# Attention output products of a two-layer encoder trunk: three rounded passes in place of fp32, with the probabilities and values split into high and low parts

## The chip, the cores and the metric

The kernel runs on one core of a Trainium2 chip. The metric is the device time in microseconds (us) of one execution. PE is TensorE, ACT is ScalarE, DVE is VectorE, POOL is GpSimd and SP is SyncE; PEld is TensorE's loading of weights.

## The reference

Two request groups of 256 and 512 tokens go through the same two layers of width 1024. Each layer has a mixer (a Hyena part and a Mamba-2 part), a cross-attention into 256 memory tokens of each group, and a squared-ReLU MLP. The change is in the cross-attention alone:

```
def memory_cross_attention(u, mem_n, w_q, w_kv, w_o):
    q = (u @ w_q).reshape(b, L, XA_HEADS, XA_HEAD_DIM)           # 4 heads of 256
    kv = (mem_n @ w_kv).reshape(b, m, 2, XA_HEADS, XA_HEAD_DIM)  # m = 256
    k, v = kv[:, :, 0], kv[:, :, 1]
    s = jnp.einsum("bqhd,bkhd->bhqk", q.astype(f32), k.astype(f32)) * (XA_HEAD_DIM ** -0.5)
    a = jax.nn.softmax(s, axis=-1)
    o = jnp.einsum("bhqk,bkhd->bqhd", a, v.astype(f32)).reshape(b, L, D_MODEL).astype(u.dtype)
    return o @ w_o
```

The outputs are fp32.

## The kernel before

Both groups are laid side by side as one axis of T = 768 tokens (6 tiles of 128; SEGS are the columns 0 to 256 and 256 to 768). Activations lie with the features on the partitions. Every engine has its own program, written out by hand in the order in which it is to run; engines wait for one another by semaphores alone. An engine that waits holds up all that stands behind in its list.

Most products of the kernel take operands that are split in two rounded parts (F32R, "hi" and "lo", lo = value - hi). The helper `three` issues three matmuls, hi x hi, hi x lo and lo x hi, into one PSUM bank. Other products, among them the scores and the output products of the attention, take fp32 operands with one call, which the chip's program holds as two instructions.

The attention of a layer runs over four heads. TensorE's list for head h is:

- T(h), line 1527: 12 transposes of the normalised probabilities `prob` into `tr_bank(0)`, `tr_bank(1)` (the two banks of PSUM tensor G[0]) and `tr_bank(2)` (a bank of M[1]). It waits for `p_nrm` (normalised) and for `o_lo` of the first output of head h-1, since that output lies in G[0].
- S(h+1), line 1060: 12 products for the scores of the next head, into M, for heads 0 to 2.
- O(h), line 1538: 8 products of `vt` (values, stationary) and `probT` (moving) into G[0] and G[1], 4 of 256 and 4 of 512 columns. They wait for `p_tc`. In the last head the two 256-column halves come first.

ScalarE's list for head h is: three copies of the transposed probabilities into `probT` (line 888, `p_tc`), the six exponentials of head h+1 (line 857, each followed by the reading of its sum), then B_hi of both outputs (line 894, waits for `o_mm`). Ahead of head 0 stand eight halves of weight chunks (lines 881 and 882) that the products behind the attention use.

VectorE's list is: the softmax of head h+1 (line 2150 maximum, 2151 scaling, 2156 reciprocal, 2157 normalisation, in the order maximum 0, maximum 1, normalise 0, maximum 2, normalise 1, normalise 2), then B_lo of both outputs (line 2196, waits for `o_hi`, raises `o_lo`). Behind the last head TensorE waits for `o_lo` and goes on with weight tiles (line 1108).

Of the kernel before, what the change touches and what calls it, by code (L numbers as in the profile page):

```python
# [21 lines left out]
F32R = mybir.dt.float32r  # L22
ALU = mybir.AluOpType
# [4 lines left out]
P = 128  # L28
# [83 lines left out]
def build_trunk(nc, xT, memT, wstream, dft, fw3, params, consts, yT):  # L112
    ctx = ExitStack()
    with ctx:
# [90 lines left out]
        qfa = place("qfa", [P, 6, T], oE + 12288)  # L205
        qfb = place("qfb", [P, T], oA + 45056)
        prob = [place(f"prob{i}", [P, TT, NMEM], oA + 32768 + 6144 * i) for i in range(2)]
        probT = [place(f"probT{i}", [P, 2, T], oE + 32768 + 6144 * i) for i in range(2)]

        relu = [place(f"relu{i}", [P, T], oE + 3072 * i) for i in range(2)]  # L210
        hidf = [place(f"hidf{i}", [P, T], oE + 6144 + 3072 * i) for i in range(2)]
# [89 lines left out]
        def par_(name, i=0, n=1, rows=P):  # L301
# [21 lines left out]
        xg_mix, xg_mlp = sem("xg_mix"), sem("xg_mlp")  # L323
        st_sum, st_var, st_std, st_rc, st_bc, st_rbc = (sem(n) for n in (
            "stat_sum", "stat_var", "stat_std", "stat_rcol", "stat_bc", "stat_rbc"))
        pre_sq = sem("pre_square")
        wdt_h, wdt_l, dt_mm = sem("wdt_hi_done"), sem("wdt_lo_done"), sem("dt_taken")
        dt_p, dt_f, dt_t = sem("dt_product"), sem("dt_scaled"), sem("dt_turned")
        conv_x, silu_d = sem("conv_for_silu"), sem("silu_done")
# [231 lines left out]
        def _(act):  # L561
# [44 lines left out]
                act.activation(A_hi[:, m, :], X[:, m, :], ACT.Copy, scale=c_("g_first", m, m + 1)).then_inc(g_hi, 1)  # L606
            first_chunk(1)
            for m in range(KT):
                act.activation(x_sq[:, m, :], X[:, m, :], ACT.Square).then_inc(pre_sq, 1)


            for L in range(DEPTH):
# [210 lines left out]
                for m in range(16):  # L823
# [16 lines left out]
                    if m in (3, 15):  # L840
# [5 lines left out]
                        for t in range(4):  # L846
                            act.activation(vt[:, t, h * 512:(h + 1) * 512], MB[t], ACT.Copy,
                                           scale=rmem[:, t:t + 1]).then_inc(v_ev, 1)

                def exps(h):  # L850

                    for i in range(3):
                        act.wait_ge(sc_max, L * 12 + (3 * h + i + 1))
                        if h >= 2:
                            act.wait_ge(p_t, L * 12 + (3 * (h - 2) + i + 1))
                        for t in (2 * i, 2 * i + 1):
                            act.activation(prob[h % 2][:, t, :], sc_bank(h, t), ACT.Exp, bias=stat[:, 2, t:t + 1],
                                           scale=1.0 / 16.0, accum_out=stat[:, 3, t:t + 1]).then_inc(p_exp, 1)

                for i in range(28):  # L860
                    p, n = divmod(i, 7)
                    bank = (GB, MB)[p % 2]
                    act.wait_ge(u_mm, L * 112 + i + 1)
                    if i < 24:
                        query_high(i + 4)
                    if n == 0:
                        if L or p:
                            act.wait_ge(q_ev, 3 * (L * 4 + p))
                        act.activation(p_one, bank[0][:, 0:HALF_T], ACT.Copy).then_inc(u_p1, 1)
                    if n == 1:  # L870
                        act.activation(p_five, bank[1][:, 0:HALF_T], ACT.Copy).then_inc(u_p5, 1)
                    if n == 4:
                        act.activation(q_at(2 * p)[:, 0:HALF_T], bank[0][:, 0:HALF_T], ACT.Copy).then_inc(u_c11, 1)
                    if i == 23:
                        act.preload_act_table(ACT.Exp)
                        exps(0)
                for s in range(2):
                    act.wait_ge(raw_in[s], 16 * (L * LOADS[s] + Q_LOADS + IN_RAW[s] + 1))
                    for h in range(2):
                        part = slice(h * 512, (h + 1) * 512)  # L880
                        act.activation(wlo[:, s, part], raw[:, s, part], ACT.Copy, scale=-1.0).then_inc(neg_done, 1)
                        act.activation(whi[:, s, part], raw[:, s, part], ACT.Copy).then_inc(hi_done, 1)
                for h in range(XH):
                    for i in range(3):
                        act.wait_ge(p_t, L * 12 + (3 * h + i + 1))
                        if h >= 2 and i == 0:
                            act.wait_ge(o_mm, L * 8 + 2 * (h - 1))
                        act.activation(probT[h % 2][:, :, i * 256:(i + 1) * 256],
                                       tr_bank(i).rearrange("p (k t) -> p k t", k=2), ACT.Copy).then_inc(p_tc, 1)
                    if h + 1 < XH:  # L890
                        exps(h + 1)
                    for i in range(2):
                        act.wait_ge(o_mm, L * 8 + (2 * h + i + 1))
                        act.activation(B_hi[:, 2 * h + i, :], G[i][:, 256:1024], ACT.Copy).then_inc(o_hi, 1)
# [171 lines left out]
        def _(pe):  # L1066
# [61 lines left out]
            for L in range(DEPTH):  # L1128
# [339 lines left out]
                stat_sum(4, mem_acc, GB[0])  # L1468
                def query_sum():

                    pe.wait_ge(v_ev, L * 8 + 4)
                    pe.wait_ge(acc_step, L * 24 + 9)
                    stat_sum()

# [9 lines left out]
                for j in range(28):  # L1484
# [6 lines left out]
                    if p == 0 and n == 6:  # L1491
                        pe.wait_ge(c_lo, L * 56 + 28)
                    if p == 1 and n == 0:
                        pe.wait_ge(v_ev, L * 8 + 8)
                    if p >= 2 and n < 4:
                        pe.wait_ge(*((u_c11, V - 1), (q_ev, 3 * Q - 4), (q_ev, 3 * Q - 3), (u_u1, V - 1))[n])
                    if n >= 4:
# [16 lines left out]
                for h in range(XH):  # L1514
                    if h:

                        pe.wait_ge(o_lo, L * 8 + (2 * h - 1))
                        pe.wait_ge(p_tc, L * 12 + 3 * h)
                    for i in range(3):
                        if h == 0 and i == 2:  # L1520
                            pe.wait_ge(q_ev, 12 * (L + 1))
# [11 lines left out]
                    def output(i, seg):  # L1533

                        a, b = SEGS[seg]
                        c0 = h * XD + i * P
                        for kt in range(2):
                            last = mm(G[i][:, 256 + a:256 + b], vt[:, 2 * seg + kt, c0:c0 + P],  # L1538
                                      probT[h % 2][:, kt, a:b], start=(kt == 0), stop=(kt == 1))
                        return last  # L1540

                    if h + 1 < XH:
                        pe.wait_ge(p_tc, L * 12 + (3 * h + 3))
                        for i in range(2):
                            if h and i:
                                pe.wait_ge(o_lo, L * 8 + 2 * h)
                            output(i, 0)
                            output(i, 1).then_inc(o_mm, 1)
                    else:
                        pe.wait_ge(p_tc, L * 12 + (3 * h + 1))  # L1550
                        output(0, 0)
                        pe.wait_ge(o_lo, L * 8 + 2 * h)
                        output(1, 0)
                        pe.wait_ge(p_tc, L * 12 + (3 * h + 3))
                        for i in range(2):
                            output(i, 1).then_inc(o_mm, 1)

# [62 lines left out]

            pe.wait_ge(acc_step, DEPTH * 24)
            stat_sum()
            pe.wait_ge(sq_done, DEPTH * 24)
            stat_sum(TT, sq, MB[1])
            stat_bcast(DEPTH * NORMS + 1, rcol)

# [4 lines left out]
        def _(dve):  # L1631
# [28 lines left out]

            def add_square(n, m):

                dve.wait_ge(sq_done, n + 1)
                if m == 0:
                    dve.tensor_copy(acc[:, 0:T], sq[:, 0:T]).then_inc(acc_step, 1)
                else:
# [37 lines left out]
                    op0=ALU.mult, op1=ALU.subtract).then_inc(xg_mix, 1)  # L1704
            first_low(1)
            for m in range(1, KT):
                dve.wait_ge(pre_sq, m + 1)
                ins = tt(acc[:, 0:T], x_sq[:, 0, :] if m == 1 else acc[:, 0:T], x_sq[:, m, :], ALU.add)
                if m < KT - 1:
                    link(ins)  # L1710
# [5 lines left out]
            for L in range(DEPTH):  # L1716
# [451 lines left out]
                for i in range(28):  # L2168
# [19 lines left out]
                            maximum(0, k)  # L2188
                    if 24 <= i < 27:
                        normalise(0, i - 24)  # L2190
                for h in range(XH):
                    if h + 1 < XH:
                        softmax(h + 1)
                    for i in range(2):
                        dve.wait_ge(o_hi, L * 8 + (2 * h + i + 1))
                        tt(B_lo[:, 2 * h + i, :], G[i][:, 256:1024], f(B_hi[:, 2 * h + i, :]), ALU.subtract).then_inc(o_lo, 1)  # L2196
# [338 lines left out]
```

## Time and profile before

| | |
|---|---|
| median of 3 timed runs | 2411.59 us (2411.05 to 2411.73) |
| the profiled execution's own time | 2412.7 us |
| its span, first to last instruction | 2410.8 us |
| mean granted TensorE clock | 0.996 |
| busy share PE, PEld, DVE, ACT, POOL | 99%, 86%, 54%, 46%, 16% |

The span is that of the profiled execution. Its own time is 1.9 us longer, and 1.1 us over the median of the timed runs. A busy share is an average over all stages. The chain that ended last is followed back from the last instruction, at each step to what released it.

### The profile page before, as it was taken

How to read it: one execution, taken by the hardware profiler on the slowest of the kernel's cores; microseconds unless marked ns; L12 is line 12 of the kernel's file. 1: busy time of each engine (PE TensorE's matmuls, PEld its weight loads, DVE VectorE, ACT ScalarE, POOL GpSimd, SP SyncE). 2: the span in 40 equal slices, each digit the busy share in tenths (PEclk: the TensorE clock that was granted, in tenths of full speed). 3: DMA queues.
4: the chain of work that ended last, by engine and by line, in shares of the span. 5: the costliest groups of instructions: out<-in, count | busy, mean ns of one | idle time of the engine just before them, and what ended most of it. 6: DMA issues, size and time to landing. Idle time of an engine off the chain costs nothing.

```text
span 2410.8 us, 33119 instructions
## 1 busy us (share of the span) xinstructions
PE 2386.5 (99%) x12908; PEld 2068.4 (86%) x12908; DVE 1311.6 (54%) x2070; ACT 1119.8 (46%) x2167; POOL 395.9 (16%) x456
## 2 busy tenths in 40 slices
PE   8999999999999999999999999999999999999997
PEld 6888668898888999989888885788988889999996
DVE  8877575375325452626368776734753265344353
ACT  5544435455445453536445435355454454435352
POOL 1111002210112121212111110022001221212121
PEclk9999999999999999999999999999999999999998
DMA  5544336852355565565555553288315565655564
GB/s 159 111 97 105 88 96 138 176 124 62 76 121 122 125 134 123 127 129 117 108 120 108 103 118 88 61 178 175 95 44 109 119 126 119 129 130 125 117 132 104
DMA packets 111863, 279.48 MB, mean 116 GB/s; under 512 B 12694, under 2 KB 12950, under 8 KB 111716
## 3 DMA queue, kind: packets, MB, share of 16 engines
q0 software_dynamic: 65088, 118.52, 29.8%
q1 hardware_dynamic: 46628, 158.93, 22.1%
q8 instruction: 101, 1.65, 0.3%
q14 instruction: 46, 0.38, 0.1%
HBM read 274.25 MB, written 3.15 MB: 115 GB/s over the span
## 4 chain that ended last, share of the span: by engine, by line
PE 97%; DMA 1%; DVE 1%; issue 0%; ACT 0%; DVEq 0%; POOL 0%; SPq 0%; ACTq 0%
PE G L1108 55%; PE M L1608 2%; PE G L1608 2%; PE M L1609 2%; PE G L1609 2%; PE M L1610 2%; PE G L1610 2%; PE M L1327 2%; PE G L1538 2%; PE M L1071 2%; PE M L1073 2%; PE M L1072 2%; PE M L1060 1%; PE G L1340 1%; PE M L1395 1%; PE G L1305 1%
## 5 line engine op out<-in xcount | busy, mean ns | idle before, releaser
L535 POOL DMA_DIRECT2D wlo<-wstream x376 | 330.0, 881 | 1541.9 <-ACT wlo L568 1304.6
L568 ACT ACTIVATE wlo<-raw 128x512 fp32r<-128x512 f32 x344 | 216.5, 629 | 654.3 <-PE G L1108 584.7
L1108 PE MATMUL G<-B_lo,whi 128*128 128x256 f32 (+1 forms) x1280 | 433.7, 339 | 0.0
L1108 PE MATMUL G<-B_hi,whi 128*128 128x256 f32 (+1 forms) x1280 | 406.0, 339 | 0.4 <-DVE B_lo L2196 0.3
L1108 PE MATMUL G<-A_lo,whi 128*128 128x256 f32 x1120 | 376.9, 341 | 0.0
L1108 PE MATMUL G<-A_hi,whi 128*128 128x256 f32 x1120 | 359.8, 345 | 10.9 <-DVE A_lo L1703 8.9
L1674 DVE TENSOR_TENSOR X<-X,G 128x768 f32<-128x768 f32 x94 | 89.6, 953 | 452.6 <-PE G L1108 357.0
L1108 PE MATMUL G<-B_hi,wlo 128*128 128x256 f32 (+1 forms) x1280 | 325.8, 336 | 0.0
L1108 PEld LDWEIGHTS G<-B_hi,wlo 128*128 128x128 f32 x1280 | 240.5, 188 | 58.2
L1108 PE MATMUL G<-A_hi,wlo 128*128 128x256 f32 x1120 | 285.8, 336 | 0.0
L1108 PEld LDWEIGHTS G<-B_lo,whi 128*128 128x128 f32 x1280 | 241.3, 189 | 27.3
L1108 PEld LDWEIGHTS G<-A_hi,wlo 128*128 128x128 f32 x1120 | 212.0, 189 | 50.5
L1108 PEld LDWEIGHTS G<-B_hi,whi 128*128 128x128 f32 x1280 | 241.4, 189 | 2.4 <-DVE B_lo L2196 2.0
L1108 PEld LDWEIGHTS G<-A_lo,whi 128*128 128x128 f32 x1120 | 212.3, 190 | 21.9
L1108 PEld LDWEIGHTS G<-A_hi,whi 128*128 128x128 f32 x1120 | 213.1, 190 | 16.1 <-issue 12.9
L569 ACT ACTIVATE whi<-raw 128x512 fp32r<-128x512 f32 x344 | 212.1, 617 | 0.0
L548 POOL DMA_DIRECT2D w_low<-wstream x72 | 62.3, 892 | 326.6 <-ACT w_low L930 315.5
L1608 PE MATMUL G<-mlp_hi,whi 128*128 128x384 f32 x336 | 113.5, 338 | 0.0
L1608 PE MATMUL M<-mlp_hi,whi 128*128 128x384 f32 x336 | 113.5, 338 | 0.0
L1609 PE MATMUL M<-mlp_lo,whi 128*128 128x384 f32 x336 | 113.3, 337 | 0.0
L1609 PE MATMUL G<-mlp_lo,whi 128*128 128x384 f32 x336 | 113.2, 337 | 0.0
L1742 DVE SCALAR_TENSOR_TENSOR tap<-pad,par,tap 128x770 f32<-128x770 f32 x104 | 106.2, 1021 | 3.7
(438 smaller groups left out, 4325.4 us busy)
## 6 DMA issues: line engine op xcount, KB each, us to landing
raw<-wstream SPq DMA_DIRECT2D x228, 512.0 KB, 4.0
wlo<-wstream POOLq DMA_DIRECT2D x376, 256.0 KB, 5.3
w_low<-wstream POOLq DMA_DIRECT2D x72, 256.0 KB, 4.2
raw_b<-wstream SPq DMA_DIRECT2D x24, 512.0 KB, 6.5
ring<-dft SPq DMA_DIRECT2D x12, 512.0 KB, 3.4
mraw<-memT SPq DMA_DIRECT2D x16, 256.0 KB, 3.2
X<-xT SPq DMA_DIRECT2D x8, 384.0 KB, 6.7
win<-dft SPq DMA_DIRECT2D x6, 512.0 KB, 4.8
```

Source lines behind the costliest of these rows:

```text
L535: pool.dma_start(low, wstream[stream(L, c)][:, part], accum_op=ALU.add).then_inc(lo_in[c % 2][h], 16)
L548: pool.dma_start(w_low[i][:, :], wstream[w + 2 * p + row][:, col * 512:(col + 1) * 512], accum_op=ALU.add).then_inc(u_lo[i], 16)
L568: act.activation(wlo[:, s, part], raw[:, s, part], ACT.Copy, scale=-1.0).then_inc(neg_done, 1)
L569: act.activation(whi[:, s, part], raw[:, s, part], ACT.Copy).then_inc(hi_done, 1)
L1071: mm(out, a_hi, b_hi, start=start, stop=False)
L1072: mm(out, a_hi, b_lo, start=False, stop=False)
L1108: last = mm(out, w, p[:, k, a:b], start=(k == 0 and w is w_hi and p is parts[0]), stop=(k == KT - 1 and (w is w_lo and only is None or onl ...
L1608: mm(out, w_hi, src[0][:, k, :], start=(n < 4 and k == 0), stop=False, skip_group_check=n > 3)
L1609: mm(out, w_hi, src[1][:, k, :], start=False, stop=False, skip_group_check=n > 3)
L1610: last = mm(out, w_lo, src[0][:, k, :], start=False, stop=(k == 3), skip_group_check=n > 3)
L1674: tt(X[:, m, :], X[:, m, :], PS[tp][:, 256:1024], ALU.add).then_inc(psum_free, 1)
L1742: ins = stt(out=dst[:, 0:n], in0=p[:, first + k:first + k + n], scalar=w(k), in1=dst[:, 0:n], op0=ALU.mult, op1=ALU.add)
```

## The change

The output products become three rounded passes each. `probT` becomes a pair `p_hi`, `p_lo`, and the values become `v_hi[h]` (one buffer per head) and `v_lo` (written over `vt`). ScalarE's copies of the turned probabilities now round (`probT_hi`); `value_high` on ScalarE rounds the values of one head, and `value_low` and `turned_low` on VectorE make the low parts. TensorE waits for the new semaphore `p_tl`, which counts the low parts. The first layer's early squares use `square_done` in place of a semaphore of their own.

```diff
-        probT = [place(f"probT{i}", [P, 2, T], oE + 32768 + 6144 * i) for i in range(2)]
+        probT = [tuple(place(f"probT_{n}{i}", [P, 2, T], o + 6144 * i, F32R) for n, o in (("hi", oE + 32768), ("lo", oE)))
+                 for i in range(2)]
+        v_hi = [place(f"v_hi{i}", [P, 4, XD], oE + 12288 + 6144 * (i % 3), F32R) for i in range(XH)]
+        v_lo = place("v_lo", [P, 4, D], oA + 16384, F32R)
...
-                act.activation(x_sq[:, m, :], X[:, m, :], ACT.Square).then_inc(pre_sq, 1)
+                act.activation(x_sq[:, m, :], X[:, m, :], ACT.Square).then_inc(sq_done, 1)
...
+                def value_high(h):
+
+                    act.activation(v_hi[h][:, :, :], vt[:, :, h * XD:(h + 1) * XD], ACT.Copy).then_inc(v_ev, 1)
...
+                act.wait_ge(v_ev, L * 12 + 8)
+                value_high(0)
...
-                        act.activation(probT[h % 2][:, :, i * 256:(i + 1) * 256],
+                        act.activation(probT[h % 2][0][:, :, i * 256:(i + 1) * 256],
                                        tr_bank(i).rearrange("p (k t) -> p k t", k=2), ACT.Copy).then_inc(p_tc, 1)
                     if h + 1 < XH:
                         exps(h + 1)
+                        value_high(h + 1)
...
+                        p_hi, p_lo = probT[h % 2]
                         for kt in range(2):
-                            last = mm(G[i][:, 256 + a:256 + b], vt[:, 2 * seg + kt, c0:c0 + P],
-                                      probT[h % 2][:, kt, a:b], start=(kt == 0), stop=(kt == 1))
+                            last = three(G[i][:, 256 + a:256 + b], v_hi[h][:, 2 * seg + kt, i * P:(i + 1) * P],
+                                         v_lo[:, 2 * seg + kt, c0:c0 + P], p_hi[:, kt, a:b], p_lo[:, kt, a:b], kt == 0, kt == 1)
...
-                        pe.wait_ge(p_tc, L * 12 + (3 * h + 3))
+                        pe.wait_ge(p_tl, L * 16 + 4 * h + 4)
...
+                def value_low(h):
+
+                    cols = slice(h * XD, (h + 1) * XD)
+                    dve.wait_ge(v_ev, L * 12 + 8 + h + 1)
+                    tt(v_lo[:, :, cols], vt[:, :, cols], f(v_hi[h][:, :, :]), ALU.subtract).then_inc(p_tl, 1)
+
+                def turned_low(h, i):
+
+                    dve.wait_ge(p_tc, L * 12 + (3 * h + i + 1))
+                    part = slice(i * 256, (i + 1) * 256)
+                    tt(probT[h % 2][1][:, :, part], tr_bank(i).rearrange("p (k t) -> p k t", k=2),
+                       f(probT[h % 2][0][:, :, part]), ALU.subtract).then_inc(p_tl, 1)
+
+                value_low(0)
                 for h in range(XH):
+                    for i in range(3):
+                        turned_low(h, i)
                     if h + 1 < XH:
                         softmax(h + 1)
+                        value_low(h + 1)
                     for i in range(2):
                         dve.wait_ge(o_hi, L * 8 + (2 * h + i + 1))
```

ScalarE's list from head 0's probabilities to head 1's, first layer, before:

```order
L888 ACTIVATE probT_126<-G 128x2x256 x2
L888 ACTIVATE probT_126<-M 128x2x256
L857 ACTIVATE prob_125,stat<-M,stat 128x256 x6
L894 ACTIVATE B_hi<-G 128x768 x2
L888 ACTIVATE probT_127<-G 128x2x256 x2
```

and now, starting with the first of the new roundings and the first of the eight weight halves behind it:

```order
L855 ACTIVATE v_hi_130<-vt 128x1024
L890 ACTIVATE wlo<-raw 128x512
...
L897 ACTIVATE probT_hi_126<-G 128x2x256 x2
L897 ACTIVATE probT_hi_126<-M 128x2x256
L864 ACTIVATE prob_125,stat<-M,stat 128x256 x6
L855 ACTIVATE v_hi_131<-vt 128x1024
L904 ACTIVATE B_hi<-G 128x768 x2
L897 ACTIVATE probT_hi_128<-G 128x2x256 x2
```

A rounding of values now stands ahead of the eight weight halves, and one between the exponentials and B_hi.

VectorE's list from the last query sum (`rbc`) to head 0's B_lo, first layer, before:

```order
L2183 TENSOR_TENSOR rbc<-acc,M 128x384
L2150 TENSOR_REDUCE stat<-M 128x2
L2151 TENSOR_SCALAR stat<-stat 128x2
L2150 TENSOR_REDUCE stat<-M 128x2
L2151 TENSOR_SCALAR stat<-stat 128x2
L2156 RECIPROCAL stat<-stat 128x2
L2157 TENSOR_TENSOR prob_125<-prob_125,stat 128x512
L2150 TENSOR_REDUCE stat<-M 128x2
```

and now the same place, with the end of the softmax and what follows it:

```order
L2194 TENSOR_TENSOR rbc<-acc,M 128x384
L2206 TENSOR_TENSOR v_lo<-vt,v_hi_130 128x4x256
L2212 TENSOR_TENSOR probT_lo_127<-G,probT_hi_126 128x2x256 x2
L2212 TENSOR_TENSOR probT_lo_127<-M,probT_hi_126 128x2x256
L2161 TENSOR_REDUCE stat<-M 128x2
L2162 TENSOR_SCALAR stat<-stat 128x2
...
L2167 RECIPROCAL stat<-stat 128x2
L2168 TENSOR_TENSOR prob_125<-prob_125,stat 128x512
L2206 TENSOR_TENSOR v_lo<-vt,v_hi_131 128x4x256
L2224 TENSOR_TENSOR B_lo<-G,B_hi 128x768 x2
```

The low parts of head 0's turned probabilities now stand ahead of head 1's maxima, and the low part of head 1's values ahead of head 0's B_lo.

## Rows read from the trace of the kernel before

**Rows 1.** The page: busy time of each engine, and the chain by engine
```profile
PE 2386.5 (99%) x12908; PEld 2068.4 (86%) x12908; DVE 1311.6 (54%) x2070; ACT 1119.8 (46%) x2167; POOL 395.9 (16%) x456
...
PE 97%; DMA 1%; DVE 1%; issue 0%; ACT 0%; DVEq 0%; POOL 0%; SPq 0%; ACTq 0%
```

**Rows 2.** The chain, first layer's attention: start us, us, engine, line, count
```profile
576.08 0.87 PE G L1527 x8
...
577.39 5.18 PE M L1060 x24
582.57 5.16 PE G L1538 x16
587.73 0.87 PE G L1527 x8
...
612.43 3.73 PE G L1538 x12
...
616.17 0.82 ACT B_hi L894
...
617.02 0.97 DVE B_lo L2196
...
618.03 12.02 PE G L1108 x68
```

**Rows 3.** The timeline of TensorE, weight tile behind the attention: start us, length us
```profile
619.18 0.28 PE L1108 MATMUL G<-B_hi,whi 128*128 128x256 f32 x1
619.30 0.28 PE L1108 MATMUL G<-B_lo,whi 128*128 128x256 f32 x1
619.42 0.40 PE L1108 MATMUL G<-B_hi,whi 128*128 128x512 f32 x1
619.65 0.40 PE L1108 MATMUL G<-B_lo,whi 128*128 128x512 f32 x1
```

**Rows 4.** The timeline of ScalarE, heads 0 and 1
```profile
576.16 0.63 ACT L881 ACTIVATE wlo<-raw 128x512 fp32r<-128x512 f32 x1 [3.70 <-PE M L1507]
...
580.34 1.05 ACT L888 ACTIVATE probT<-G 128x512 f32<-128x512 f32 x2
...
591.74 0.47 ACT L857 ACTIVATE prob<-M,stat 128x256 f32<-128x256 f32 x1 [1.69 <-DVE stat L2151]
...
592.20 0.47 ACT L857 ACTIVATE prob<-M,stat 128x256 f32<-128x256 f32 x1
592.56 0.20 ACT L857 ACTIVATION_READ_ACCUMULATOR prob<-M,stat 128x1 f32 x1
```

**Rows 5.** The timeline of VectorE, softmax of head 1
```profile
579.16 0.69 DVE L2150 TENSOR_REDUCE stat<-M 128x2 f32<-128x512 f32 x1 [2.48 <-PE M L1060]
...
583.02 0.69 DVE L2157 TENSOR_TENSOR prob<-prob,stat 128x512 f32<-128x512 f32 x1
583.63 0.68 DVE L2150 TENSOR_REDUCE stat<-M 128x2 f32<-128x512 f32 x1
...
584.43 0.16 DVE L2156 RECIPROCAL stat<-stat 128x2 f32<-128x2 f32 x1
584.62 0.69 DVE L2157 TENSOR_TENSOR prob<-prob,stat 128x512 f32<-128x512 f32 x1
```

**Rows 6.** Groups by shape, ScalarE and VectorE: busy us, mean ns, idle before
```profile
L569 ACT ACTIVATE whi<-raw 128x512 fp32r<-128x512 f32 x344 | 212.1, 617 | 0.0
L909 ACT ACTIVATE B_hi<-hidf 128x768 fp32r<-128x768 f32 x16 | 13.5, 847 | 0.5
L1954 DVE TENSOR_TENSOR hpa<-G,win 128x1024 f32<-128x1024 f32 x6 | 7.3, 1218 | 4.0 <-PE G L1305 4.0
```

**Rows 7.** The chain in the second layer's input projection (L1177: 16 columns each)
```profile
1256.84 1.44 PE M L1177 x12
1258.28 7.81 PE G L1108 x35
```

**Rows 8.** Busy time of each engine and TensorE's clock, the 2 us from 1258
```profile
1258.00:1260.00 2.00, 2.00 (x9) 1.78 (x9) 1.93 (x3) 0.00 (x0) 0.00 (x0) 0.62 0.91 240
```

More of the change, by code:

```diff
@@ L325, in build_trunk @@
             "stat_sum", "stat_var", "stat_std", "stat_rcol", "stat_bc", "stat_rbc"))
-        pre_sq = sem("pre_square")
+        p_tl = sem("prob_turned_low")
         wdt_h, wdt_l, dt_mm = sem("wdt_hi_done"), sem("wdt_lo_done"), sem("dt_taken")
@@ L1469, in query_sum @@
                 def query_sum():
-                    pe.wait_ge(v_ev, L * 8 + 4)
+                    pe.wait_ge(v_ev, L * 12 + 4)
                     pe.wait_ge(acc_step, L * 24 + 9)
@@ L1493, in _ @@
                     if p == 1 and n == 0:
-                        pe.wait_ge(v_ev, L * 8 + 8)
+                        pe.wait_ge(v_ev, L * 12 + 8)
                     if p >= 2 and n < 4:
@@ L1517, in _ @@
                         pe.wait_ge(o_lo, L * 8 + (2 * h - 1))
-                        pe.wait_ge(p_tc, L * 12 + 3 * h)
+                        pe.wait_ge(p_tl, L * 16 + 4 * h)
                     for i in range(3):
@@ L1549, in _ @@
                     else:
-                        pe.wait_ge(p_tc, L * 12 + (3 * h + 1))
+                        pe.wait_ge(p_tl, L * 16 + 4 * h + 2)
                         output(0, 0)
@@ L1553, in _ @@
                         output(1, 0)
-                        pe.wait_ge(p_tc, L * 12 + (3 * h + 3))
+                        pe.wait_ge(p_tl, L * 16 + 4 * h + 4)
                         for i in range(2):
@@ L1622, in _ @@
             stat_sum()
-            pe.wait_ge(sq_done, DEPTH * 24)
+            pe.wait_ge(sq_done, KT + DEPTH * 24)
             stat_sum(TT, sq, MB[1])
@@ L1661, in add_square @@
             def add_square(n, m):
-                dve.wait_ge(sq_done, n + 1)
+                dve.wait_ge(sq_done, KT + n + 1)
                 if m == 0:
@@ L1706, in _ @@
             for m in range(1, KT):
-                dve.wait_ge(pre_sq, m + 1)
+                dve.wait_ge(sq_done, m + 1)
                 ins = tt(acc[:, 0:T], x_sq[:, 0, :] if m == 1 else acc[:, 0:T], x_sq[:, m, :], ALU.add)
```

## The prediction

> **What bounds the kernel now.** The page comes first: TensorE is busy 99% of the span and 97% of the chain that ended last, while VectorE is busy 54% and ScalarE 46% [rows 1]. Read alone, that says that anything taken off TensorE is gained whole. But a busy share is a mean over stages, so I read the chain of the attention stage of the first layer, in order of time [rows 2]. With T(h) the transposes of head h's probabilities, S(h+1) the scores of the next head and O(h) the output products, the reader is to see T(0) at 576.08, S(1) at 577.39, O(0) at 582.57 and T(1) at 587.73: 11.65 us a head, O being 5.16 of it, and TensorE never stopping. The last head is different: after its first 12 output instructions (3.73 us) the chain goes to ScalarE (B_hi, 0.82) and VectorE (B_lo, 0.97) before the next weight tile can start at 618.03. So in this stage TensorE bounds, with two short lists of work, ScalarE's and VectorE's, running beside it in a fixed order. Each hands TensorE something that it needs: probT before O(h), normalised probabilities and B_lo(h,0) before T(h+1), since the transposes write where output 0 stood.
>
> **The products.** Before, O(h) is 8 fp32 products, 16 instructions, 5.16 us [rows 2]. After, it is 24 rounded ones, 12 of 256 and 12 of 512 columns. The kernel already does such passes: from start to start 0.12 us at 256 columns and 0.23 at 512 [rows 3]. So 12 x 0.12 + 12 x 0.23 = 4.20 us, good to 0.1 by the two digits of the rows. Saved: 0.96 a head, 7.7 us for 8 heads, if nothing else moves.
>
> **The splits.** Four pieces are added per head on the two other engines. (a) turned_low, three 128x512 subtractions on VectorE that read PSUM; the normalisations of the same shape are 0.69 long and let the next start after 0.61 (583.02 to 583.63) [rows 5]. (b) value_high, one 128x1024 rounding on ScalarE. No row has it; 128x512 takes 0.617 and 128x768 0.847 [rows 6], so 1.08 by the same slope, and the next instruction starts 0.09 before that ends. Bounds: 0.85 (it can't be under the 768 one) and 2 x 0.617 = 1.23. (c) value_low, one 128x1024 subtraction, 1.22 by the row of that shape [rows 6], next start after 1.14. (d) The retiring of the old copy: probT_hi is rounded where probT was copied, same shape, nothing. The merged semaphore (x_sq on square_done) moves no work: nothing, and if it were late it would show at the very start only.
>
> **Head 0.** I walk the trace's clock with the new order. ScalarE is free at 576.16 and does value_high(0) first; the eight weight splits that stood there (576.16 to 580.34, 0.52 each [rows 4]) and the probT copies behind them move by 0.99 or so, so the copies end 581.9, 582.4, 583.0. Delaying the weight splits costs nothing by itself: their tiles are used from 618. VectorE now does turned_low(0, 0 to 2) before the maxima of head 1, each behind its copy: start 581.94, end 583.85. TensorE, ready at 582.57, waits for the last; I add 0.2 for the first result after a pause (12 instructions took 3.73 at 612.43 where two thirds of 5.16, their share of the columns, is 3.44, so up to 0.29) [rows 2]. O(0) runs 584.09 to 588.30.
> The maxima, first at 579.16 before [rows 5], now begin at 583.77. A maximum with its scaling takes 0.80 (583.63 to 584.43), a normalisation 0.19 + 0.61 (584.43, 584.62 [rows 5]), a pair of exponentials 1.02 until VectorE may go on (591.74 to 592.56 + 0.20) with the next ScalarE instruction 0.9 after the pair's start [rows 4]. Maximum 0 and 1 end the wait at 585.37; the first pair is done at 585.69, normalisation 0 to 586.56, maximum 2 ready 587.44, its pair done 588.50, last normalisation done 589.43. value_high(1) sits behind that pair: 588.38 to 589.47. value_low(1): 589.50, B_lo(0,0) may start 590.64 and ends 591.60. T(1) then starts at 591.84 instead of 587.73: **4.1 us lost**, with TensorE idle from 588.30 for 3.5 of them. The products' gain of this head is inside that pause.
>
> **Heads 1 and 2.** From S(h+1)'s end the path is: last maximum and scaling 0.06 + 0.92, pair of exponentials up to value_high 0.94, value_high 1.08, value_low's 1.17, B_lo's 0.96, hand-over 0.2: 5.3 us. Before, T(h+1) followed S by 5.16; the cheaper O(h) alone would allow 4.20. So O's gain is not only unused, the head takes 6.5 + 5.3 = 11.82 instead of 11.65. turned_low is off this path here: it ends 3.2 us after T starts, and S runs for 5.2. Cost: 2 x 0.17 = 0.3.
>
> **Head 3.** No softmax and no values are left. T(3) starts, B_lo(2,1) ends 0.7 later, three turned_low behind it end 3.2 after T's start. The first two 256-column outputs go between, then output 0's long half ends 5.1 after T's start, B_hi 0.82 and B_lo 0.97: next tile 6.93 after T(3), against 618.03 - 611.03 = 7.00 before [rows 2] (611.03 is 587.73 + 2 x 11.65). Nothing.
>
> Sum: 4.1 + 0.3 - 0.1 = 4.4 us a layer, 8.8 for two, taking the second layer alike. value_high is the one priced without a row, and it stands on this path four times (before the weight splits and once per head after): at its low bound a layer costs 4.4 - 4 x 0.23 = 3.5, at its high one 4.4 + 4 x 0.15 = 5.0.
>
> **The clock.** TensorE was granted 0.62 of its clock from 1258 to 1260 [rows 8], a stretch at 1.2 GHz, after 12 matmuls of 16 columns that had filled 1.44 us [rows 7]. The 35 matmuls behind it took 7.81 us; at the 12.02/68 = 0.177 us of the row at 618.03 [rows 2] they would take 6.19: 1.6 us lost. The pause before T(1) is 3.5 us with no matmul at all, more than twice as long as that thin stretch, and only transposes follow. I take it that the clock falls once there in each layer, and since TensorE's scores stand on the path of head 1, the 1.6 us are paid: 3.2 us. Bounds: 0 (no fall) and 3 falls a layer, 9.7.
> The Trainium skill (TensorE: Matmul & The Clock Gate, Why this matters for your kernels) advises against idle gaps between bursts of matmuls because the clock then goes back to its lower level; it speaks against this change, which makes such a gap. By that rule the time is 2423.6, without it 2420.4.
>
> **Time.** The profiled execution took 2412.7 for a span of 2410.8; the sum added to it is 2412.7 + 8.8 + 3.2 = 2424.7. The median of the timed runs is 1.1 lower, so **2423.6**.
>
> **Rivals.**
> - A, chain as above but the clock stays at 2.4 GHz: 2411.6 + 8.8 = 2420.4. For it: the transposes and the wait ahead of 612.43 are a short thin stretch too, and the 12 instructions behind it show no halving (3.73 for 3.44). Chance 0.24.
> - B, my forecast, one fall a layer: 2423.6. Chance 0.48.
> - C, more falls or a dearer value_high: 2426 to 2430. Chance 0.11.
> - D, the splits are mostly covered: no change. If value_high and value_low took 1.1 us together instead of 2.3, the same walk gives 1.7 a layer (B_lo then waits for its product) and 2415. Even with all splits free it gains only 0.9 a layer, 2410, because the last maximum, its exponentials and B_lo still stand between S and T(h+1). Chance 0.12.
> - E, faster: the whole 7.7 us is kept, 2404. Mechanism: the path from the last score to T(h+1) is shorter than 4.2 us, that is 1.1 less than my 5.3, and head 0's maxima are not held up. For it: VectorE is idle nearly half of the span [rows 1]. Against it: those idle times are not at this place. Chance 0.05.
>
> **Numbers.** 0.2%, about what a measurement of this kernel can tell, is 4.8 us: 2406.8 to 2416.4. Slower is A, B, C and a little of D: 0.83. Same is most of D: 0.12. Faster is E: 0.05. The range for 8 in 10 leaves out E, most of D and the far end of C: 2416 to 2429.
>
> **What would show it.** In the profile after: matmuls of probT_hi with v_hi at 0.12 and 0.23 apart; B_hi(0,0) on ScalarE behind value_high(1), about 3 us after its product is done; TensorE idle some 3.5 us before T(1) with VectorE's B_lo as releaser; T to T 11.8 in heads 2 and 3; a granted clock under 1.00 in the 4 us behind T(1) in both layers. If TensorE has no pause before T(1), or the value splits cost half, the step on head 0 is wrong; if the clock row stays 1.00, it is A. More than 0.3 us in turned_low's 0.69 would show as a longer pause before O(0).

## The result and the profile after

The changed kernel takes 2424.59 us (median of 4 runs, 2422.54 to 2425.86), the kernel before 2411.66 beside it (4 runs, 2411.05 to 2412.66): ratio 1.0055, 95% interval 1.0044 to 1.0067. It is slower by 12.9 us, where 12.0 were forecast.

The profiled execution took 2425.43 us for a span of 2423.7. The page's busy times and its chain by engine, answering to [rows 1]:

```profile
PE 2385.8 (98%) x12972; PEld 2077.7 (86%) x12972; DVE 1335.8 (55%) x2102; ACT 1128.5 (47%) x2175; POOL 396.0 (16%) x456
...
PE 95%; DVE 2%; ACT 1%; DMA 1%; issue 0%; DVEq 0%; SPq 0%; ACTq 0%
```

TensorE's busy time is 0.7 us less and the time 12.9 us more: TensorE waits where it did not wait before. (Busy time counts a matmul at half rate as longer, so it doesn't show the 7.7 us that the products were to save.) Where, the chain of the first layer's attention tells (start us, us, engine, line, count), answering to [rows 2]. T is line 1537 now, S 1070, the three passes of O 1081 to 1083, value_high 855, value_low 2206, turned_low 2212, B_lo 2224.

```profile
575.04 1.06 ACT v_hi L855
576.10 0.52 ACT wlo L890
...
580.77 1.89 DVE probT_lo L2212 x3
582.65 0.61 DVE stat L2161
...
586.28 1.02 ACT prob L864 x4
587.30 0.95 ACT v_hi L855
...
588.27 1.23 DVE v_lo L2206
589.50 0.88 DVE B_lo L2224
...
590.42 1.28 PE G L1537 x8
591.71 0.85 PE M L1537 x4
592.56 6.26 PE M L1070 x24
...
603.93 1.09 PE G L1537 x8
...
615.76 0.67 PE G L1537 x4
...
620.95 0.82 ACT B_hi L904
...
621.80 0.97 DVE B_lo L2224
...
622.81 1.31 PE G L1118 x6
```

From 575.04 to 590.42 there is not one TensorE row on the chain. It runs over value_high(0), the eight weight halves, the copies and turned_low on to head 1's maxima, exponentials, value_high(1), value_low(1) and B_lo(0,0); before, TensorE's own work filled the same stretch. The waits of TensorE in the whole trace (us in total, times, longest) name the releasers:

```profile
PE G L1537 <- DVE B_lo L2224: 10.1, 6, 3.2
...
PE G L1081 <- DVE probT_lo L2212: 3.6, 4, 1.3
```

The rest is the granted clock. Windows of 2 us in both layers (length, PE busy, PEld, DVE, ACT, POOL, then the clock, the DMA share and GB/s):

```profile
588.00:590.00 2.00, 0.00 (x0) 0.00 (x0) 1.95 (x3) 1.64 (x3) 0.00 (x0) 1.00 0.03 4
590.00:592.00 2.00, 1.58 (x11) 1.58 (x12) 1.48 (x3) 0.86 (x2) 0.00 (x0) 0.80 0.00 0
592.00:594.00 2.00, 2.00 (x7) 1.69 (x6) 1.75 (x3) 0.94 (x2) 0.00 (x0) 0.50 0.00 0
594.00:596.00 2.00, 2.00 (x9) 1.69 (x8) 0.60 (x1) 0.00 (x0) 0.00 (x0) 0.85 0.00 0
1784.00:1786.00 2.00, 0.00 (x0) 0.00 (x0) 1.85 (x3) 2.00 (x4) 0.00 (x0) 0.96 0.59 107
1786.00:1788.00 2.00, 0.85 (x4) 0.85 (x5) 1.96 (x3) 0.37 (x1) 0.00 (x0) 0.50 0.00 0
1788.00:1790.00 2.00, 2.00 (x11) 2.00 (x10) 0.90 (x2) 1.20 (x2) 0.00 (x0) 0.50 0.03 8
1790.00:1792.00 2.00, 2.00 (x6) 1.55 (x6) 1.17 (x2) 0.60 (x1) 0.00 (x0) 0.50 0.02 4
1792.00:1794.00 2.00, 2.00 (x9) 1.72 (x8) 0.83 (x2) 0.00 (x0) 0.00 (x0) 0.83 0.00 0
```

A 0.50 is the level of 1.2 GHz. It holds for some 3 us in the first layer and for about twice that in the second. The two falls don't start at the same point. In the first layer the clock is still at 1.00 when T(1) starts and falls some 0.8 us into the transposes (the mean of 591.0 to 591.5 is 0.69). In the second it falls in the pause itself, some 1.3 us before T(1) starts at 1787.15 (0.85 in 1785.5 to 1786.0).

**The account of the span.** I call "stage" the time from the end of the last query product to the start of the next weight tile. The first layer's went from 41.95 us (576.08 to 618.03 [rows 2]) to 47.84 (574.97 to 622.81), the second's from 41.95 (1767.05 to 1809.00) to 48.86 (1771.71 to 1820.57): 5.89 and 6.91. What lies ahead is 1.11 shorter, what lies between 0.12 shorter, what lies behind 1.33 longer, and the sum is the 12.9 by which the span grew. The change touches nothing there but the semaphore of experiment 8. The granted clock, which fell in the trace of before between 60 and 80 us, did not in this one, and in the last stage it fell further (the 12 matmuls of line 1127 took 2.43 us where the same ones took 1.51).

### The profile page after: what moved, and what is told of

It reads as the page before. It is cut to its first block, busy times and chain, and to the rows that moved or that the text cites. A ratio compares the mean times of both kernels' runs of the same rounds, so it can differ in the third digit from the quotient of the medians.

```text
span 2423.7 us, 33287 instructions
## 1 busy us (share of the span) xinstructions
PE 2385.8 (98%) x12972; PEld 2077.7 (86%) x12972; DVE 1335.8 (55%) x2102; ACT 1128.5 (47%) x2175; POOL 396.0 (16%) x456
## 4 chain that ended last, share of the span: by engine, by line
PE 95%; DVE 2%; ACT 1%; DMA 1%; issue 0%; DVEq 0%; SPq 0%; ACTq 0%
PE G L1118 55%; PE M L1619 2%; PE G L1619 2%; PE M L1620 2%; PE G L1620 2%; PE M L1621 2%; PE G L1621 2%; PE M L1337 2%; PE M L1081 2%; PE M L1083 2%; PE M L1082 2%; PE G L1350 1%; PE M L1405 1%; PE M L1070 1%; PE G L1315 1%; PE M L1058 1%
```

## The experiments

Theory M: the time of this stage is set by the chains through ScalarE's and VectorE's lists, plus TensorE's clock after the pause that they make. Rivals: the passes themselves cost more than priced; turned_low alone is the cost; any added work on the two engines costs in proportion, wherever it stands. "At full clock" means the stage with the price of a fall taken off, or of a trace in which none came. The kernel before ran beside each group of kernels on the same chip: 2410.44 us (21 runs) beside the first four, 2411.25 (24 runs) beside the next four, 2411.18 (21 runs) beside the last two. The stages of all of them stand in a table behind the last experiment.

**1. TensorE kept busy in the pause.** The changed kernel, and behind the output products of head 0:

```diff
+                        if h == 0:
+                            for n in range(12):
+                                mm(MB[3], v_hi[0][:, 0, 0:P], probT[0][0][:, 0, 0:512], start=True, stop=True)
```

> The changed kernel with 12 unused matmuls of 512 columns (2.8 us) put into TensorE's pause between head 0's output products and head 1's transposes, in both layers; they write a PSUM bank that is free there. My theory: the clock falls in that pause, and the fall costs what the changed kernel took over the chain of waits, so with TensorE kept busy the granted clock stays at 1.00 there, T(1) is not later, and the time falls from 2424.6 to about 2420.5. Rival: the clock follows something else, or its fall costs nothing because the other engines bound the stage: then 2424 to 2425, or more by what the extra matmuls cost.

Measured: 2421.05 us (2420.02 to 2421.89), ratio 1.0041 (1.0027 to 1.0055). Its chain, first layer (T, then S at full speed, then T(2)):

```profile
592.09 1.09 PE G L1537 x8
593.18 0.44 PE M L1537 x4
593.62 5.20 PE M L1070 x24
...
603.92 1.09 PE G L1537 x8
```

and its window there has the clock at full:

```profile
592.00:594.00 2.00, 1.91 (x15) 1.86 (x16) 1.49 (x3) 1.22 (x3) 0.00 (x0) 1.00 0.00 0
```

T(1) comes 15.46 us after the query products (15.45 in the changed kernel), so the added matmuls delay nothing. T(1) with S(2) takes 6.73 us instead of 8.40. The stage is 46.17 us in both layers: the falls had cost 1.67 and 2.69, and the chain without them costs 4.22 a layer. (Over the kernel before beside it the median is 10.6 us, more than the 8.4 of the two stages; its interval, 6.5 to 13.3, holds both. Against the 12.9 of the changed kernel that is 2.3 less, where the two stages of the traces give 4.36: the size of the fall's price comes from the traces, the medians only agree in sign.) With the pause filled the clock falls in neither layer, so the idle TensorE is what lets it fall. That such a pause always brings a fall isn't shown, and experiments 2 and 4 speak against it.

**2. The products back in fp32, all splits kept** (the fp32 products read the rounded high parts):

```diff
-                            last = three(G[i][:, 256 + a:256 + b], v_hi[h][:, 2 * seg + kt, i * P:(i + 1) * P],
-                                         v_lo[:, 2 * seg + kt, c0:c0 + P], p_hi[:, kt, a:b], p_lo[:, kt, a:b], kt == 0, kt == 1)
+                            last = mm(G[i][:, 256 + a:256 + b], v_hi[h][:, 2 * seg + kt, i * P:(i + 1) * P].bitcast(F32),
+                                      p_hi[:, kt, a:b].bitcast(F32), start=(kt == 0), stop=(kt == 1))
```

> The changed kernel with all its splits on ScalarE and VectorE, but the output products as fp32 again (of the rounded high parts alone, so the low parts are made and not used). My theory: the products' saving is nearly all hidden behind the path last maximum, exponentials, value_high, value_low, B_lo, so 0.96 us a head more on TensorE adds only about 0.8 a layer: 2422 without a fall of the clock, up to 2426 with falls, against 2424.6. Rival: TensorE bounds the stage and the products save 0.96 a head: then 7.7 more than the changed kernel, 2432.

Measured: 2422.62 us (2420.72 to 2423.22), ratio 1.0046 (1.0033 to 1.006). In the second layer, where its clock stayed at full, the stage is 47.24. So with the splits in place the rounded products save 47.24 - 46.17 = 1.07 us a layer, where four times 0.96 = 3.8 come off TensorE's work: nearly three quarters of it fall into pauses. The rival, by which TensorE bounds the stage and all of it would be lost again (2432), is out.

**3. The products alone.** The low parts are left out, of values and of probabilities. The values are rounded as they leave PSUM, the waits are the old ones, and `three` gets the rounded values and the rounded probabilities in every pass:

```diff
-                            last = three(G[i][:, 256 + a:256 + b], v_hi[h][:, 2 * seg + kt, i * P:(i + 1) * P],
-                                         v_lo[:, 2 * seg + kt, c0:c0 + P], p_hi[:, kt, a:b], p_lo[:, kt, a:b], kt == 0, kt == 1)
+                            last = three(G[i][:, 256 + a:256 + b], vt[:, 2 * seg + kt, c0:c0 + P],
+                                         vt[:, 2 * seg + kt, c0:c0 + P], p_hi[:, kt, a:b], p_hi[:, kt, a:b], kt == 0, kt == 1)
...
-                value_low(0)
...
-                        turned_low(h, i)
```

> The three rounded passes alone: values rounded as they leave PSUM and used for high and low, probabilities rounded in the old copy and used for high and low, no value_high, value_low or turned_low, old waits; the low parts are left out. My theory: with the old lists on the other engines the products' saving comes through, 0.95 in heads 1 and 2 and most of it in head 3, nothing in head 0 whose B_lo is late already: 2.6 a layer, 2406.5. Rival 1: the passes are dearer than I took them (more weight loads): 2411 or more. Rival 2: all 0.96 x 8 is kept: 2404.

Measured: 2405.09 us (2402.9 to 2407.21), ratio 0.9977 (0.9968 to 0.9986); stage 39.35, that is 2.60 below before. The three passes are cheaper than fp32, as priced, and the rival of dearer passes is gone. The other rival, that all 7.7 us are kept, gives 2404, and the median alone only just leaves it out (3.4 to 7.7 us below the kernel before); the stage, 2.6 below and not 3.8, is what speaks against it. Even here 1.2 us a layer of the 3.8 are not gained. Half of that is T(1), which still waits for B_lo,

```profile
584.88 0.88 DVE B_lo L2217
585.81 1.09 PE G L1534 x8
```

which is 11.34 us after the query products' end (574.47), where 11.65 - 0.96 = 10.69 would be free of waits. T(2) follows 10.93 behind it (the first transposes after the pause take 1.09 us, not 0.87), T(3) 10.7 behind T(2), and the last head saves 0.6: its first product starts here, 1.37 us after T(3) at 607.47.

```profile
608.84 0.39 PE G L1078
```

**4. The values not split** (turned_low kept; the low part of the values is left out, and rounded values stand in place of v_hi and v_lo):

```diff
-                value_high(0)
...
-                        value_high(h + 1)
...
-                value_low(0)
...
-                        value_low(h + 1)
```

> The changed kernel without value_high and value_low (values rounded as they leave PSUM, used for high and low), with turned_low kept: the low part of the values is left out. My theory: of the 4.4 us a layer of the chain, the values' split stands for 4.0: 0.4 a layer remain, 2412.5, plus up to 3 if the clock falls in the pause before T(1), which shrinks from 3.5 to 2.2 us. Rival: turned_low, which TensorE waits for by name, is the cost: then 2418 or more.

Measured: 2413.83 us (2410.56 to 2416.04), ratio 1.0011 (1.0002 to 1.002). Stage 42.36 in the first layer, 43.99 in the second, where the clock fell; the expectation was 2412.5 and up to 3 more for a fall, and the rival's 2418 is out. turned_low therefore adds 42.36 - 39.35 = 3.0 us a layer. Of it 1.9 are in head 0: T(1) comes at 587.78, 13.22 after the query products, where experiment 3 has 11.34. T(2), 10.93 later (598.71), and T(3) at 609.44 are as far apart as there. The other 1.1 are in head 3: turned_low(3,0) stands in VectorE's list behind B_lo of head 2, and the first output product waits for it, 2.48 us after T(3) instead of 1.37.

```profile
610.31 0.96 DVE B_lo L2219
611.27 0.61 DVE probT_lo L2209
...
611.92 0.39 PE G L1078
```

**5. The values' splits alone** (turned_low is left out, and in the second pass the rounded probabilities stand in for their low parts):

```diff
-                                         v_lo[:, 2 * seg + kt, c0:c0 + P], p_hi[:, kt, a:b], p_lo[:, kt, a:b], kt == 0, kt == 1)
+                                         v_lo[:, 2 * seg + kt, c0:c0 + P], p_hi[:, kt, a:b], p_hi[:, kt, a:b], kt == 0, kt == 1)
...
                 value_low(0)
                 for h in range(XH):
-                    for i in range(3):
-                        turned_low(h, i)
```

> The kernel before with the values' splits of the change alone: ScalarE writes every head's rounded value columns and VectorE their differences, in the change's places and buffers; the probabilities' low parts are not computed, and the rounded probabilities serve in their place in the second pass (low parts of the probabilities are left out of the output; in their place the rounded probabilities count a second time). So this is the change without turned_low. Theory (the lists of ScalarE and VectorE set the pause before T(1) and the pitch of the heads): value_high and value_low still lie between the last exponential and B_lo(0,0), so T(1) is held by B_lo, about 2.5 us after the output products end instead of 3.2 in the changed kernel; with products 0.96 us a head shorter a layer comes to 1.6 us over before, 2413.6 us in all, and up to 3 us more if TensorE's granted clock falls in those pauses as it did in the changed kernel. Rival 1 (turned_low is what costs): 2405, as with the products alone. Rival 2 (the output products' passes set the time): 2403 to 2405 too. If the theory holds, this and the run without the value splits (2413.8) each lie between products alone (2405.1) and the changed kernel (2424.6), and the two splits' costs nearly add: 8.5 and 8.7 above products alone, 17 together plus the clock.

Measured: 2418.3 us (2412.96 to 2421.88), ratio 1.0028 (1.0017 to 1.0038). That is 1.7 us above the end of what I had allowed; 0.8 of it is that the kernel before was at 2411.25 here and not at 2410.4. The chain's pieces are there as expected,

```profile
586.00 0.96 ACT v_hi L855
...
586.98 1.22 DVE v_lo L2209
588.20 0.88 DVE B_lo L2225
...
589.13 1.54 PE G L1538 x8
590.67 0.85 PE M L1538 x4
591.53 6.00 PE M L1070 x24
```

T(1) and S(2) take 8.40 us instead of 6.73 at full clock: 1.67 for the fall, in both layers. The stage is 45.21, or 43.5 with that taken off, 1.6 over before as the walk had it. Both splits hurt by themselves, so the rival "turned_low is what costs" falls. At full clock they add 4.2 (43.5 - 39.35) and 3.0 us a layer to the products alone, and 6.8 together (46.17 - 39.35). Clock and stage make 6.5 of the 7.0 us; the rest lies outside the attention and within the scatter.

**6 and 7. The same work in another order, without and with matmuls in the pause.** value_high(h+1) ahead of the exponentials, value_low(h+1) behind the first maximum, and the second weight chunk's four roundings (`output_chunk(1)`) behind head 1's exponentials. Nothing is computed differently; three of the four buffers of rounded values lie elsewhere:

```diff
                     if h + 1 < XH:
+                        value_high(h + 1)
                         exps(h + 1)
-                        value_high(h + 1)
+                        if h == 0:
+                            output_chunk(1)
...
                     maximum(h, 0)
+                    if low:
+                        value_low(h)
                     maximum(h, 1)
```

> The changed kernel with nothing computed differently, but the two value splits moved out of the chain after the last exponential: value_high(h+1) stands ahead of the exponentials of head h+1 on ScalarE, value_low(h+1) behind the first row maximum on VectorE, and the rounding of the second chunk of output weights behind head 1's exponentials instead of ahead of head 0's. Theory (chain through the two lists): the path last maximum, exponentials, B_hi, B_lo in heads 1 and 2 gets shorter, their pauses go to 0 and 0.4 us, but in head 0 the later start of the exponentials and maxima makes the pause before T(1) about 4.4 us instead of 3.2; by sums of the rows a layer comes to 2.0 us over before instead of 4.4, so 2414.5 us with no clock fall and 2417 to 2420 with falls as in the changed kernel. Rival (the amount of work that ScalarE and VectorE carry sets the time, not where it stands): 2424 as the changed kernel.

> The run before this one with 12 matmuls of 512 columns added between the output products of head 0 and the turning of head 1 (their result is not read), so that TensorE is not idle in that pause. Theory: 2414.5 us, no fall of TensorE's granted clock at the start of head 1. If moved early alone is at the same time, the falls cost nothing there; if it is 2 to 5 us above this one, that is their price. Rival (fill delays turning): above moved early alone.

Measured: 2420.64 us (2417.96 to 2421.36), ratio 1.0039 (1.0025 to 1.0053), and with the added matmuls 2415.56 (2413.47 to 2417.47), ratio 1.0019 (1.001 to 1.0028). Both medians lie above what was expected, 0.6 us above the end of 2417 to 2420 and 1.1 above 2414.5, and 0.8 of that is the kernel before, as in experiment 5. Not one instruction fewer than in the changed kernel, and the stage at full clock is 43.94 instead of 46.17, 2.0 over before as expected. The chain of the second of the two, first layer: T(1), S(2), T(2), S(3).

```profile
589.87 1.09 PE G L1542 x8
590.96 0.44 PE M L1542 x4
591.40 5.18 PE M L1075 x24
...
600.80 0.88 PE G L1542 x8
601.68 0.44 PE M L1542 x4
602.12 5.18 PE M L1075 x24
```

S(2) to S(3) takes 10.72 us: 11.65 less the products' 0.96. Head 1's gain is whole once its splits stand under TensorE's scores. Head 0 is still where it loses: T(1) comes 14.80 us after the query products, against 15.45 in the changed kernel and 11.65 before, and since O(0) starts earlier than in the changed kernel the wait for B_lo is longer (4.1 us in the trace without the filling, 3.2 in the changed kernel). The chain of that trace shows one reason: the four roundings of the second weight chunk now stand between head 1's exponentials and B_hi(0,0), from 586.38 to 588.45. Head 3 loses 0.5 (7.47 us from T(3) at 611.54 to the next tile, 7.00 before). Without the filling the stages are 46.24 and 45.62: the clock takes 2.30 and 1.68. With the same amount of work the order alone takes 2.2 us a layer off, so the third rival, cost in proportion wherever the work stands, falls. (That the amount counts too is what experiments 3 to 5 show. Experiment 6 without the filling isn't clear of the changed kernel by the medians, 9.4 us over before against 12.9; the stages carry the comparison.)

**8. One semaphore for the squares**, the part of the change that was priced at nothing:

```diff
-        pre_sq = sem("pre_square")
...
-                act.activation(x_sq[:, m, :], X[:, m, :], ACT.Square).then_inc(pre_sq, 1)
+                act.activation(x_sq[:, m, :], X[:, m, :], ACT.Square).then_inc(sq_done, 1)
```

> The kernel before with one part of the change alone, that nobody has priced: the squares ahead of the first layer and those of the layers count on one semaphore. Theory: no instruction or wait moves, same time as before (2410 to 2412). Rival: if it is off by more than 1 us the account of the other runs has to carry it.

Measured: 2411.28 us (2408.18 to 2414.36) against 2411.25, ratio 1.0002 (0.9993 to 1.0011). Nothing that a measurement can tell, and the stages are those of before.

**9. The change in head 2 alone**, and **10. in heads 1 to 3**, both with the splits ahead of where the change has them, as in experiment 6 (in 9 value_low even stands ahead of the first maximum), and with all eight weight halves ahead of head 0 again. The core of the first:

```diff
+                        if h == 1:
+                            value_high(2)
                         exps(h + 1)
...
+                            if h != 2:
+                                last = mm(G[i][:, 256 + a:256 + b], vt[:, 2 * seg + kt, c0:c0 + P],
+                                          probT_full[h % 2][:, kt, a:b], start=(kt == 0), stop=(kt == 1))
+                                continue
...
-                        softmax(h + 1)
-                        value_low(h + 1)
+                        softmax(h + 1, h == 1)
```

> The kernel before with the change in head 2 alone: heads 0, 1 and 3 keep their fp32 output products, values and probabilities; head 2's value_high stands ahead of its exponentials, its value_low ahead of its first row maximum. Theory (what counts is whether a split lies between the last maximum and B_lo, or delays TensorE past the pause it has anyway): in head 2 the splits have the scores of head 3 as cover, no pause grows, and the 0.96 us that the rounded products save stays: 2409.4 us where the kernel before has 2411.25, ratio 0.9992, so by itself too small for the measurement, and the pitch from head 2's to head 3's turning goes from 11.65 to 10.7 us in the trace. Rival (any split that ScalarE and VectorE carry costs in proportion, 14.9 us over products alone and the clock shared by four heads): 0.96 saved and some 2 us a layer lost, 2413.5, pitch over 12.

> The run with the splits moved early (2420.6), with the change left out in head 0: head 0's products, values and probabilities stay in fp32, and its three turned_low, its two value splits and its part of the order go. Theory (head 0 is where that version loses, since the weight chunks' roundings and the splits stand in one row there): the pause before T(1) falls from 4.4 to 1.95 us, a layer comes to 0.55 us over before, so 2412.4 us with the clock at full speed, 2412 to 2416 with falls. Rival (the loss is spread over the heads, a quarter each of the 9.4 us over before): 2418.

Measured: 2409.45 us (2407.32 to 2410.47), ratio 0.9993 (0.9983 to 1.0002), and 2411.74 (2410.83 to 2414.01), ratio 1.0005 (0.9996 to 1.0014), beside 2411.18. Neither differs from before by what a measurement can tell. The trace can: the chain of the first, with T(2), S(3) and the end of the stage,

```profile
598.61 0.87 PE G L1545 x8
599.48 0.44 PE M L1545 x4
599.92 5.18 PE M L1075 x24
...
609.08 0.25 PE G L1088
...
610.70 3.73 PE G L1558 x12
...
616.31 8.81 PE G L1123 x49
```

has O(2) ending at 609.33, so T(3) 10.7 us after T(2), and a stage of 41.01, 0.94 under before in both layers. Its trace lies 1.9 us below the kernel before in the two stages, and its median 1.7, but the interval reaches over 1, so it isn't shown to be faster. The rival's 2413.5 is outside its runs. Leaving the change out in head 0 alone took experiment 6's version from 9.4 us over before to 0.6, where the rival of four equal shares has 2418, 7 over. By the traces 4.0 of those 8.8 us are the falls of the clock, which this one doesn't have, and 3.1 are the two stages at full clock (43.94 and 42.41); the rest lies outside the stages.

| Kernel | stage, layer 1 | layer 2 | clock in the stage |
|---|---|---|---|
| before | 41.95 | 41.95 | full |
| changed | 47.84 | 48.86 | fell in both |
| 1, changed and matmuls in the pause | 46.17 | 46.17 | full |
| 2, fp32 products, all splits | 48.91 | 47.24 | fell in layer 1 |
| 3, products alone | 39.35 | 39.34 | full |
| 4, no value splits | 42.36 | 43.99 | fell in layer 2 |
| 5, value splits alone | 45.21 | 45.21 | fell in both |
| 6, splits moved | 46.24 | 45.62 | fell in both |
| 7, splits moved and matmuls in the pause | 43.94 | 43.94 | full |
| 8, one semaphore | 41.95 | 41.95 | full |
| 9, head 2 alone | 41.01 | 41.01 | full |
| 10, heads 1 to 3 | 42.41 | 42.42 | full |

## Why the prediction was right, step by step

Times after the query products' end let the trace of before and of after be laid on one another; experiment 1 shows the chain without the clock.

- **The products.** Priced at 4.20 us for 24 passes and 0.96 saved. O(0) in the changed kernel starts one pass every 0.12 and 0.23 us; pitches of 10.72 and 10.7 in experiments 7 and 9, for 11.65, give 0.93 to 0.95. Right, and right that most of it would fall into pauses.
- **The splits.** value_high, which no row of before had, takes 1.055 us (8 instructions), forecast 1.08; value_low 1.226, forecast 1.22; turned_low 0.69, x3 in 1.89 us of chain, forecast 1.91. The Trainium skill (VectorE: DVE Perf Modes, The TRN2 errata) has a formula for ScalarE with source and result in SBUF, 224 cycles and one per element at 1.2 GHz; worked out from it, value_high is 1.04 us, an estimate. The trace agrees to 0.02.
- **Head 0.** O(0) was to start 8.01 us after the query products (584.09 less 576.08) and started 7.74 after (582.71 less 574.97); T(1) was to come at 15.76 and came at 15.45; the pause 3.5 and 3.2. Of the 0.2 us that I added for O(0)'s restart about 0.1 shows: its first passes start at 582.71, 582.93 and 583.05. All of the order was right: ScalarE began B_hi(0,0) at 588.14, 3.06 us after its product's end (forecast about 3).
- **Heads 1 and 2.** 11.82 a head forecast, 11.83 each in experiment 1 (592.09, 603.92, 615.75). That it fits to 0.01 is luck: T and S take 6.73 us, not 6.5, since the first transposes after a wait take 1.09 and not 0.87, and the path behind S takes 5.10 (598.82 to 603.92), not 5.3, since value_high holds it up for 0.96 and B_lo for 0.88, not 1.08 and 0.96. The mechanism, that path and no other, is right.
- **Head 3.** 6.93 forecast, 7.05 measured (615.75 to 622.80), 7.00 before. Nothing, as forecast, but as the sum of two things that the prediction did not price apart: without turned_low the head takes 6.35 (experiment 3), and waiting for it takes that gain back.
- **Sum.** 4.4 a layer forecast, 4.22 measured, 8.4 instead of 8.8 for both.
- **The clock.** One fall a layer was right for the profiled execution, its price was not: 1.6 us each forecast, 1.67 in layer 1 and 2.69 in layer 2, 4.4 instead of 3.2. I had taken the price from one fall [rows 7, 8], and that fall was not the size of every fall; the half rate in layer 2 began while TensorE was still idle and lasted twice as long. By the rule on idle gaps in the Trainium skill (TensorE: Matmul & The Clock Gate, Why this matters for your kernels) the clock falls at this place, and the trace agrees with 0.50 in the windows of both layers. The price isn't the same in every execution: two of the four had a mean granted clock of 0.994 (2425.43, the profiled one, and 2425.86 us) and two of 0.996 (2422.54 and 2423.75 us), where the kernel before has 0.996. That speaks for cheaper falls in the latter two, of which no trace was kept.
- **The time.** 8.4 + 4.4 = 12.8 in the stages, 12.9 in the medians, forecast 12.0: the two errors, 0.4 too much for the chain and 1.2 too little for the clock, are of opposite sign and partly cancel.
- **A step that was wrong and did not count.** In rival D I wrote that with all splits free only 0.9 a layer is gained, 2410. Experiment 3 gains 2.6 a layer and 5.3 in the median. The last maximum, its exponentials and B_lo do stand between S and T(h+1), but that path is shorter than the 4.20 us of the products: from the last maximum to T(1) it measures 3.7 in experiment 4 (584.08 to 587.78), and in experiment 3 neither T(2) nor T(3) waits. The heads gain 0.31, 0.72, 0.92 and 0.6 there. I had put too long a path behind the last maximum for the case without splits.
- **Rival E** (the 7.7 us kept, 2404) comes near to what the products do without their splits, 2405.09, but even there the stages keep 5.2 of the 7.7.

What stays open: why one fall of the clock lasts longer than another, and why the same pause brings one in one layer and none in the other (experiment 2 fell in the first alone, experiment 4 in the second alone). Nothing in the runs settles it.

## What to carry to other kernels

An operation made cheaper on the engine that bounds a stage pays only if what it needs from the other engines does not lengthen their chain back to it; walk their lists in order, with the row for each piece, before counting the saving. The same splits cost 4.2 us a layer behind the last exponential, 2.0 when most of them stood under the scores, and in the one head where nothing waited they let the 0.96 us through. A pause on TensorE can be charged twice, once as itself and once as the half rate behind it, so price it with more than one fall read from the trace.

## What the runs showed of the hardware

- 12 matmuls of 512 columns in a pause kept the granted clock at full and cost the chain nothing: 1.67 and 2.69 us of stage came back in the traces. The median is 2421.05 for 2424.59, of which 1.2 us is the kernel before, 2410.44 beside the one and 2411.66 beside the other.
- Falls came behind shorter pauses too: in experiment 5 TensorE waited 2.28 us for B_lo, and the first layer's transposes behind that wait took 2.39 us instead of 1.53. In experiment 10 it waited 1.66 and they took 1.53. In experiment 2 the wait was 2.28 us in both layers and in experiment 4 it was 1.95 in both, and each time the clock fell in one layer and not in the other.
- One ScalarE rounding of 128x1024 takes 1.055 us, less than twice the 0.617 of one of 128x512. The 512 further elements add 0.438, which leaves a part of 0.18 us that doesn't grow with the size (an estimate from these two).
- The first eight transposes after a wait for B_lo take 1.09 us at full clock, 0.87 where TensorE came straight from other matmuls (experiments 1 and 3 against before).
